# Two halves of one change: a shorter modulation ahead of the scans, and a memory scan whose values carry a column of ones

## The chip, the core and the metric

The kernel runs on one core of a Trainium2 chip, as one program with one launch. The metric is the device time of that core in microseconds, lower is better. Five engines work side by side: TensorE (PE), VectorE (DVE), ScalarE (ACT), GpSimd (POOL) and SyncE (SP), which here issues most transfers. Each has an instruction stream of its own, and semaphores order them.

## What is computed

Two transformer blocks follow each other. Only the first part of the first one is touched: modulation, RMS norm, the input projection, and two bidirectional chunked scans, of which the second (mLSTM, "memory") matters here.

```python
mod_x = (jax.nn.silu(c) @ ada_w + ada_b)[:, None, :]
mod_c = (jax.nn.silu(c_ctx) @ ada_w + ada_b)[None, None, :]
sh1x, sc1x, g1x, sh2x, sc2x, g2x = jnp.split(mod_x, N_MOD, axis=-1)
zx = modulate(rmsnorm(x, norm1_g), sh1x, sc1x) @ w_in
zc = modulate(rmsnorm(ctx, norm1_g), sh1c, sc1c) @ w_in
# memory scan, one chunk, per head
num = qk @ vc + w_inter[..., None] * (qc @ s)
den = jnp.sum(qk, axis=-1) + w_inter * (qc @ n)
h = num / jnp.maximum(jnp.abs(den), jnp.exp(-m_t))[..., None]
s_new = decay[..., None, None] * s + kw.T @ vc
n_new = decay[..., None] * n + jnp.sum(kw, axis=2)
x = x + g1x * mixer_output(gla_hx, ml_hx, ...)
```

Model width 1024, sequence 1024, context 256. `ada_w` is 1024 x 6144, in fp32 24 MB: six vectors of 1024, of which shift and scale of the first norm (`sh1`, `sc1`) are needed first, for x and for the context; the other four (`g1x, sh2x, sc2x, g2x`) only for x, and only behind the scans.

## The kernel before, in words

Everything is fp32; the projections are made of three fp32r products (`product3`, lines 97 to 101) of values split in a rounded high part and a rest. The layout is channels on 128 partitions (`KD = 8` tiles of them) by 1280 tokens (`TOT`, context first), in chunks of 128 (`NCH = 10`, two of context, eight latent).

The order of work is written by hand. The head is a series of stages, each closed by a barrier:

1. `modulation` (line 323). SP loads `ada_w` in 12 slabs of 2 MB (128 partitions x 8 x 512) in a ring of three; TensorE multiplies each with the two columns of `silu(c)` into two rows (8 fp32 matmuls of 512 columns, each two passes); VectorE copies the rows; 48 small transposes turn them into channels.
2. `first_norm` (line 388) loads context, x and gain, and then calls `norm_split` (line 263) once for the context and once for x. There ScalarE squares, TensorE sums the squares over the partitions with a matrix of ones, VectorE makes the reciprocal of the root, multiplies by it (line 315), ScalarE applies gain and shift twice (`y`, and `high` rounded to fp32r, line 291), and VectorE writes the rest `y - high` (line 318).
3. `first_scans` (line 1046) is one stage for the projection and both scans. The projection's weights come in 29 tiles of 512 KB (`Inputs.load`), GpSimd splits each (`Inputs.halve`, lines 446 and 448), TensorE multiplies it by the tokens in pieces of 512, 512 and 256 columns (or 2 x 512 for the gate tiles), 24 passes a piece, and ScalarE takes the bank away (`Inputs.take`). There are 79 pieces. 27 go ahead of the linear scan, 28 in its gaps, 12 between the scans and 12 in gaps of the memory scan, by two tables:

```python
LINEAR_FILLS = [(2, 1)] * 8 + [(1, 1)] * 2
MEMORY_FILLS = [(0, 0, 0)] * 2 + [(1, 0, 0), (1, 1, 0)] * 4
```

The three numbers are pieces in the chunk's three places on TensorE: behind the scores, behind the transposes of k, behind the state's step.

A chunk of the memory scan (`Memory.tensor` from line 881, `Memory.vector` from 952) goes, for both directions d and four heads: TensorE broadcasts rows of gate sums into bank `X[d]` (line 892) and q times k into `Q[d]` (898). VectorE makes the arguments of the exponentials from `X` (971 to 977), ScalarE the exponentials (938 to 940), TensorE transposes k into `X` (904), VectorE weights q, scores and k (982, 985, 988). TensorE makes the output from weighted scores and v and from weighted q and state (914, 915), and the denominator from the same left sides and one column each, `ones1` or `norm` (916, 917), in bank `Dn`. VectorE reads the denominator (991) and scales the output (1000). TensorE makes the state's step (925) and that of `norm` (926); VectorE decays and adds `norm` (1002, 1003) and the state (1005, 1006). The next chunk's rows wait for the state, as they overwrite `X`. Chunks 0 and 1 are of the context and have no output.

Of the kernel before, what the change touches and what calls it, by code (L numbers as in the profile page):

```python
# [8 lines left out]
F32 = mybir.dt.float32  # L9
# [7 lines left out]
P = 128  # L17
# [245 lines left out]
def norm_split(nc, name, src, total, high, rest, gain, shift, ones):  # L263

    cs = chunks_of(total)
    with Stage(nc, name) as s:
        sq = [s.sb(f"sq{j}", [P, BANK]) for j in range(2)]
        rs = s.sb("rs", [P, total])
        t, y = [s.sb(f"t{j}", [P, total]) for j in range(2)], [s.sb(f"y{j}", [P, total]) for j in range(2)]
        ps = [s.ps(f"p{c}") for c in range(len(cs))]  # L270
        squared, used, inverted = s.sem("squared"), s.sem("used"), s.sem("inverted")
        meant, rooted, scaled, gained, left = s.sem("meant"), s.sem("rooted"), s.sem("scaled"), s.sem("gained"), s.sem("left")
        with nc.Block() as block:
            @block.scalar
            def _(act):
                n = 0
                for a, m in cs:
                    for k in range(KD):
                        if n >= 2:
                            act.wait_ge(used, n - 1)  # L280
                        nc.scalar.activation(sq[n % 2][:, 0:m], src[:, k, a:a + m], ACT.Square).then_inc(squared, 1)
                        n += 1
                for c, (a, m) in enumerate(cs):
                    act.wait_ge(meant, c + 1)
                    nc.scalar.activation(rs[:, a:a + m], rs[:, a:a + m], ACT.Sqrt).then_inc(rooted, 1)
                for k in range(KD):
                    act.wait_ge(scaled, k + 1)
                    if k >= 2:
                        act.wait_ge(left, k - 1)
                    for out in (y[k % 2][:], high[:, k, 0:total]):  # L290
                        nc.scalar.activation(out, t[k % 2][:], ACT.Identity, bias=shift(k) if shift else 0.0, scale=gain(k)).then_inc(gained, 1)

            @block.tensor
            def _(pe):
                n = 0
                for c, (a, m) in enumerate(cs):
                    for k in range(KD):
                        pe.wait_ge(squared, n + 1)
                        nc.tensor.matmul(ps[c][:, 0:m], ones[:, 0:P], sq[n % 2][:, 0:m], start=(k == 0), stop=(k == KD - 1)).then_inc(used, 1)
                        n += 1  # L300

            @block.vector
            def _(dve):
                for c, (a, m) in enumerate(cs):
                    dve.wait_ge(used, KD * (c + 1))
                    nc.vector.tensor_scalar(rs[:, a:a + m], ps[c][:, 0:m], 1.0 / D, EPS, ALU.mult, ALU.add).then_inc(meant, 1)
                for c, (a, m) in enumerate(cs):
                    dve.wait_ge(rooted, c + 1)
                    nc.vector.reciprocal(rs[:, a:a + m], rs[:, a:a + m]).then_inc(inverted, 1)
                dve.wait_ge(inverted, len(cs))  # L310
                for k in range(KD + 1):
                    if k < KD:
                        if k >= 2:
                            dve.wait_ge(gained, 2 * (k - 1))
                        nc.vector.tensor_tensor(t[k % 2][:], src[:, k, 0:total], rs[:], ALU.mult).then_inc(scaled, 1)
# [3033 lines left out]
```

## Time and profile before

| | us |
|---|---|
| median of 3 runs (4555.51 to 4556.99) | 4555.62 |
| the profiled execution, its own time | 4557.76 |
| its span | 4556.1 |
| TensorE busy | 3954.2 (87%) |
| VectorE, ScalarE, GpSimd busy | 2163.8, 1493.4, 1078.0 |
| first product of the input projection starts at | 200.92 |
| memory scan, from its first rows to the stage's end | 659.3 to 953.3 |

The profile is of one execution. "Busy" sums the time of instructions on an engine; idle time has a releaser, the instruction or transfer whose semaphore ended it. [...] PE rows count passes: an fp32 matmul shows as two. The numbers behind the name of a line are lines of the kernel before.

### The profile page before, as it was taken

How to read it: one execution, taken by the hardware profiler on the slowest of the kernel's cores; microseconds unless marked ns; L12 is line 12 of the kernel's file. 1: busy time of each engine (PE TensorE's matmuls, PEld its weight loads, DVE VectorE, ACT ScalarE, POOL GpSimd, SP SyncE). 2: the span in 40 equal slices, each digit the busy share in tenths (PEclk: the TensorE clock that was granted, in tenths of full speed). 3: DMA queues.
4: the chain of work that ended last, by engine and by line, in shares of the span. 5: the costliest groups of instructions: out<-in, count | busy, mean ns of one | idle time of the engine just before them, and what ended most of it. 6: DMA issues, size and time to landing. Idle time of an engine off the chain costs nothing. (4 is left out here: it accounts for less than half of the span.)

```text
span 4556.1 us, 45877 instructions
## 1 busy us (share of the span) xinstructions
PE 3954.2 (87%) x17652; PEld 3102.2 (68%) x17652; DVE 2163.8 (47%) x2425; ACT 1493.4 (33%) x1866; POOL 1078.0 (24%) x578
## 2 busy tenths in 40 slices
PE   7499988948549999995788878999979899999998
PEld 1278878836437878775566656777757688888886
DVE  0346734442238888886453422222224564344335
ACT  0332110120227777772422032222222232233233
POOL 0122220013021111103232111222204344444443
PEclk9689987868659999996898789999979999999999
DMA  6131220132249999994232121121115433323323
GB/s 241 67 88 60 76 75 28 38 125 106 84 157 392 395 400 402 400 381 176 94 141 92 37 91 50 66 68 63 62 55 190 142 94 97 97 93 96 98 87 103
DMA packets 152147, 638.80 MB, mean 140 GB/s; under 512 B 18664, under 2 KB 42072, under 8 KB 135344
## 3 DMA queue, kind: packets, MB, share of 16 engines
q1 hardware_dynamic: 121904, 545.89, 33.0%
q10 hardware_dynamic: 20400, 61.35, 3.5%
q0 software_dynamic: 9680, 29.29, 1.7%
q8 instruction: 113, 1.85, 0.2%
q14 instruction: 50, 0.41, 0.0%
HBM read 532.86 MB, written 103.62 MB: 140 GB/s over the span
## 5 line engine op out<-in xcount | busy, mean ns | idle before, releaser
L2990 POOL TENSOR_TENSOR t_wl<-t_raw,t_wh 128x1024 fp32r<-128x1024 f32 (+1 forms) x176 | 397.5, 2262 | 547.1 <-ACT t_wh L3042 547.1
L99 PE MATMUL m_b<-b_high,m_high 128*128 128x512 f32 x960 | 414.6, 432 | 27.0 <-ACT m_ob L1938 19.1
L100 PE MATMUL m_b<-b_rest,m_high 128*128 128x512 f32 x960 | 393.6, 410 | 0.0
L101 PE MATMUL m_b<-b_high,m_low 128*128 128x512 f32 x960 | 384.6, 401 | 0.0
L1909 POOL TENSOR_TENSOR m_high<-m_raw,m_one 128x1024 fp32r<-128x1024 f32 x60 | 115.8, 1931 | 918.1 <-PE m_b L101 864.1
L99 PE MATMUL t_b<-b_high,t_wh 128*128 128x512 f32 x768 | 303.2, 395 | 19.7 <-POOL t_wl L2990 19.5
L100 PE MATMUL t_b<-b_rest,t_wh 128*128 128x512 f32 x768 | 300.7, 392 | 0.0
L101 PE MATMUL t_b<-b_high,t_wl 128*128 128x512 f32 x768 | 300.5, 391 | 0.0
L3042 ACT ACTIVATE t_wh<-t_raw 128x1024 fp32r<-128x1024 f32 (+1 forms) x176 | 175.6, 999 | 343.6 <-PE t_b L101 288.2
L99 PE MATMUL zs_z<-zs_hs,zs_high 128*128 128x512 f32 (+1 forms) x632 | 243.7, 386 | 38.2 <-POOL zs_low L448 38.2
L99 PEld LDWEIGHTS m_b<-b_high,m_high 128*128 128x128 f32 x960 | 187.6, 195 | 89.2 <-ACT m_ob L1938 19.5
L100 PE MATMUL zs_z<-zs_hs,zs_high 128*128 128x512 f32 (+1 forms) x632 | 235.9, 373 | 0.0
L1938 ACT ACTIVATE m_ob<-m_b 128x512 f32<-128x512 f32 x120 | 71.0, 596 | 502.4 <-PE m_b L101 494.9
L101 PE MATMUL zs_z<-zs_hs,zs_low 128*128 128x512 f32 (+1 forms) x632 | 235.1, 372 | 0.0
L100 PEld LDWEIGHTS m_b<-b_rest,m_high 128*128 128x128 f32 x960 | 188.0, 196 | 49.0 <-issue 8.2
L101 PEld LDWEIGHTS m_b<-b_high,m_low 128*128 128x128 f32 x960 | 187.1, 195 | 45.2
L1596 DVE TENSOR_TENSOR ex_wlo<-ex_raw,ex_who 128x2048 fp32r<-128x2048 f32 x78 | 178.7, 2292 | 56.1 <-ACT ex_who L1543 53.9
L99 PE MATMUL t_b<-t_hidh,t_wh 128*128 128x512 f32 x512 | 200.1, 391 | 5.0 <-DVE t_hidl L3139 5.0
L1596 DVE TENSOR_TENSOR ex_wlg<-ex_raw,ex_whg 128x2048 fp32r<-128x2048 f32 x80 | 183.2, 2292 | 43.4 <-ACT ex_whg L1543 43.2
L100 PE MATMUL t_b<-t_hidl,t_wh 128*128 128x512 f32 x512 | 199.9, 390 | 0.0
L101 PE MATMUL t_b<-t_hidh,t_wl 128*128 128x512 f32 x512 | 199.7, 390 | 0.0
L3143 DVE TENSOR_TENSOR t_x<-t_x,t_b 128x512 f32<-128x512 f32 x80 | 54.9, 686 | 290.9 <-PE t_b L101 290.7
(619 smaller groups left out, 9094.5 us busy)
## 6 DMA issues: line engine op xcount, KB each, us to landing
ex_raw<-in_expert_w SPq DMA_DIRECT2D x118, 2048.0 KB, 10.3
t_raw<-in_w_ff SPq DMA_DIRECT2D x128, 512.0 KB, 3.5
m_raw<-in_w_ug SPq DMA_DIRECT2D x60, 512.0 KB, 4.4
ada_w<-in_ada_w SPq DMA_DIRECT2D x12, 2048.0 KB, 7.7
yrows<-ex_y ACTq DMA_DIRECT2D x38, 512.0 KB, 10.9
gates<-m_ob SPq DMA_DIRECT2D x32, 512.0 KB, 2.9
me_g<-gates SPq DMA_DIRECT2D x32, 512.0 KB, 3.7
zs_raw<-in_w_in_s SPq DMA_DIRECT2D x29, 512.0 KB, 3.6
```

Source lines behind the costliest of these rows:

```text
L99: nc.tensor.matmul(out, w[0], x[0], start=first, stop=False)
L100: nc.tensor.matmul(out, w[0], x[1], start=False, stop=False)
L101: return nc.tensor.matmul(out, w[1], x[0], start=False, stop=last)
L1596: V.tensor_tensor(half(wl[u], x_), half(raw[slot], x_), half(wh[u], x_).bitcast(F32), ALU.subtract).then_inc(left, 1)
L1909: g.tensor_tensor(W.high[j][:], W.raw[j][:], W.one[:].broadcast_to([P, D]), ALU.mult).then_inc(W.rounded, 1)
L1938: self.nc.scalar.activation(self.ob[n % 2][:, c * BANK:(c + 1) * BANK], self.banks[m % len(self.banks)][:], ACT.Copy).then_inc(self.taken, 1)
L2990: self.nc.gpsimd.tensor_tensor(self.wl[u % self.NW][:, 0:m], self.raw[u % 2][:, 0:m], self.wh[u % self.NW][:, 0:m].bitcast(F32), ALU.subtr ...
L3042: S.activation(self.wh[u % self.NW][:, 0:m], self.raw[u % 2][:, 0:m], ACT.Copy).then_inc(self.rounded, 1)
L3143: V.tensor_tensor(at, at, b[:], ALU.add).then_inc(self.added, 1)
```

## The change

**The head.** `modulation`, `first_norm` and `norm_split` go. A class `Head` inside the stage of the scans takes their place. It loads context and x (in two halves of 512 tokens) first and then only the first 4 of 12 slabs, as 8 half slabs of 1 MB in a ring of three, with the first two weight tiles of the projection ahead of the last half slab. TensorE multiplies them into four banks; the squares are added by VectorE to one tile `acc`, so TensorE makes one sum of partitions per arrival (256, 512, 512 tokens) in place of eight. x is scaled by the reciprocal root before the modulation is known. Then, piece by piece of the projection (0 to 511, 512 to 1023, 1024 to 1279), VectorE applies gain and shift, ScalarE rounds, and the rest is subtracted by VectorE for even k and GpSimd for odd k. TensorE's first pieces wait for the rest of their own piece alone (`Head.ready`).

**The remaining two thirds** of `ada_w` come through the ring of the weight tiles as 32 quarters of 512 KB (128 partitions x 2 x 512), behind the 29 tiles. VectorE multiplies them by `silu(c)` of x alone (two operations a quarter, four quarters a slab into one of two accumulators), TensorE sums the partitions of each slab with four one-column matmuls, and the bias is added at the end of the scan.

**The memory scan.** v and the state are 129 wide, with a column of ones in v, so the denominator and `norm` are the 129th column of output and state. The fourth head of each direction no longer fits into its bank and goes to `EQ` (outputs, the bank of `Dn`) and `EX` (steps, the third bank of the projection, which has two banks from there on). The state's decay stands ahead of the step's wait, the step counts per direction, and the fills are moved: three pieces in each of chunks 2 to 5, none behind; eight quarters in each of chunks 6 to 9. ScalarE takes its banks behind the exponentials. The diff, cut to its core:

```diff
+class Head:
+    NT, SLABS, RING = 2 * KD, 4, 3
+    PIECES = [(0, BANK), (BANK, BANK), (2 * BANK, CTX)]
+    ARRIVALS = [(0, CTX), (CTX, BANK), (CTX + BANK, BANK)]
...
+    def load(self, sp, between):
...
+        for n in range(2 * self.SLABS):
+            if n >= self.RING:
+                sp.wait_ge(self.used, n - self.RING + 1)
+            if n == 2 * self.SLABS - 1:
+                between()
+            sp.dma_start(self.w[n % self.RING][:], self.A["ada_w"][n // 2][:, n % 2 * 4 * BANK:(n % 2 + 1) * 4 * BANK]).then_inc(self.w_in[n % self.RING], 16)
...
+    def tensor(self, pe):
+        pe.wait_ge(self.silu, 1)
+        mm_ = self.nc.tensor.matmul
+        for n in range(2 * self.SLABS):
+            if n in (1, 2, 3):
+                a, m = self.ARRIVALS[n - 1]
+                pe.wait_ge(self.gathered, (KD - 1) * n)
+                mm_(self.ps[n - 1][:, 0:m], self.C["ones"][:], self.acc[:, a:a + m], start=True, stop=True).then_inc(self.summed, 1)
+            pe.wait_ge(self.w_in[n % self.RING], 16 * (n // self.RING + 1))
+            for x in range(4):
+                k = n % 2 * 4 + x
+                mm = mm_(self.slab[n // 2][0:2, :], self.cs[:, k, :], self.w[n % self.RING][:, x * BANK:(x + 1) * BANK], start=k == 0, stop=k == KD - 1)
+            mm.then_inc(self.used, 1)
...
+    def vector(self, dve):
...
+        for i, (a, m) in enumerate(self.ARRIVALS):
+            dve.wait_ge(self.rooted, i + 1)
+            V.reciprocal(self.rs[:, a:a + m], self.rs[:, a:a + m]).then_inc(self.inverted, 1)
+            dve.wait_ge(self.inverted, i + 1)
+            for k in range(KD):
+                V.tensor_tensor(self.x[:, k, a:a + m], self.x[:, k, a:a + m], self.rs[:, a:a + m], ALU.mult).then_inc(self.scaled, 1)
+        dve.wait_ge(self.c_in, 48)
+        dve.wait_ge(self.turned, 1)
...
     def load(self, sp, n):
-        if n >= 2:
+        if n >= N_Z + 2:
+            sp.wait_ge(self.modulated, 2 * (n - N_Z - 1))
+        elif n >= 2:
             sp.wait_ge(self.split[n % 2], n // 2)
-        sp.dma_start(self.raw[n % 2][:], self.A["w_in_s"][n]).then_inc(self.w_in[n % 2], 16)
+        sp.dma_start(self.raw[n % 2][:], self.A["w_in_s"][n] if n < N_Z else self.rest(n - N_Z)).then_inc(self.w_in[n % 2], 16)
...
+            for x in range(2):
+                k, w, acc = i % 4 * 2 + x, self.raw[n % 2][:, x * BANK:(x + 1) * BANK], self.acc[s % 2][:]
+                dve.wait_ge(self.modulated, 2 * i + x)
+                if k == 0:
+                    self.nc.vector.tensor_scalar(acc, w, self.head.cs[:, k, 0:1], None, ALU.mult).then_inc(self.modulated, 1)
+                else:
+                    self.nc.vector.scalar_tensor_tensor(acc, w, self.head.cs[:, k, 0:1], acc, ALU.mult, ALU.add).then_inc(self.modulated, 1)
...
-MEMORY_FILLS = [(0, 0, 0)] * 2 + [(1, 0, 0), (1, 1, 0)] * 4
+MEMORY_FILLS = [(0, 0, 0)] * 2 + [(1, 1, 1)] * 4 + [(0, 0, 0)] * 4
+MODULATION_FILLS = [(0, 0, 0, 0)] * 6 + [(2, 2, 2, 2)] * 4
```

TensorE, one head's output in the memory scan (`zs_pa` is bank `Q[0]`, `zs_pk` is `Dn`, `ml_v` the values), before:

```order
L914 MATMUL zs_pa<-ml_v,mlb_arg 128x128
L915 MATMUL zs_pa<-mlb_state,mlb_inter 128x128
L916 MATMUL zs_pk<-mlb_ones,mlb_arg 128x1
L917 MATMUL zs_pk<-mlb_norm,mlb_inter 128x1
L914 MATMUL zs_pa<-ml_v,mlb_arg 128x128
```

and now, the same head and the next, and then the step of both directions (`zs_z` is the bank `EX`):

```order
L984 MATMUL zs_pa<-ml_v,mlb_arg 128x129
L985 MATMUL zs_pa<-mlb_state,mlb_inter 128x129
L984 MATMUL zs_pa<-ml_v,mlb_arg 128x129
...
L990 MATMUL zs_pa<-ml_v,mlb_kw 128x129 x3
L990 MATMUL zs_z<-ml_v,mlb_kw 128x129
L990 MATMUL zs_pst<-ml_v,mlb_kw 128x129 x3
L990 MATMUL zs_z<-ml_v,mlb_kw 128x129
```

The one-column matmuls are gone, two a head in the output and one in the step.

VectorE, chunk 6, from the weighted k to the next chunk's first operation (`zs_raw` holds a quarter, `mlb_acc` a slab's accumulator), now:

```order
L1054 SCALAR_TENSOR_TENSOR mlb_kw<-zs_pst,mlb_kd 128x512
L499 SCALAR_TENSOR_TENSOR mlb_acc<-zs_raw,zs_cs,mlb_acc 128x512 x4
L1059 TENSOR_TENSOR mlb_state<-mlb_state,mlb_kd 128x516 x2
...
L1073 TENSOR_TENSOR mlb_o<-zs_pk,mlb_den 128x2x128
L497 TENSOR_SCALAR mlb_acc<-zs_raw,zs_cs 128x512
L499 SCALAR_TENSOR_TENSOR mlb_acc<-zs_raw,zs_cs,mlb_acc 128x512 x3
L1078 TENSOR_TENSOR mlb_state<-mlb_state,zs_pa 128x387
L1078 TENSOR_TENSOR mlb_state<-mlb_state,zs_pst 128x387
L1079 TENSOR_TENSOR mlb_state<-mlb_state,zs_z 128x2x129
L499 SCALAR_TENSOR_TENSOR mlb_acc<-zs_raw,zs_cs,mlb_acc 128x512 x4
```

The decay (L1059) stood behind the step's wait before, and two of the four fills of a chunk show here on both sides of the state's additions.

TensorE, the head now (`hd_w` a half slab, `hd_acc` the added squares):

```order
L344 MATMUL zs_pa<-hd_w,zs_cs 2x512 x4
L340 MATMUL zs_pst<-hd_acc,all_ones 128x256
L344 MATMUL zs_pa<-hd_w,zs_cs 2x512 x4
L340 MATMUL zs_pst<-hd_acc,all_ones 128x512
L344 MATMUL zs_z<-hd_w,zs_cs 2x512 x4
L340 MATMUL zs_pk<-hd_acc,all_ones 128x512
L344 MATMUL zs_z<-hd_w,zs_cs 2x512 x20
L349 MATMUL zs_pa<-all_ident,hd_rows 128x2 x16
```

The third sum stands behind the third half slab, and 32 products of slabs are left of 96.

## Rows read from the trace of the kernel before

**Rows 1.** The page, 40 equal slices of the span, in tenths.
```profile
PE   7499988948549999995788878999979899999998
...
PEclk9689987868659999996898789999979999999999
```
**Rows 2.** Windows by stage: stretch, length, busy PE, PEld, DVE, ACT, POOL, clock, DMA.
```profile
200.90:659.30 458.40, 432.21 (x2236) 355.55 (x2237) 259.05 (x258) 111.50 (x169) 113.53 (x48) 0.95 0.24 81
659.30:953.30 294.00, 263.73 (x1488) 240.66 (x1488) 127.19 (x276) 26.16 (x64) 18.05 (x8) 0.78 0.09 31
```
**Rows 3.** Timeline of the head: start, duration, engine, line, operation, idle before.
```profile
15.12 85.39 PE L358 MATMUL ada_p<-ada_w,ada_cs 128*2 128x512 f32 x192 [15.12 <-DMA ada_w<-in_ada_w]
...
125.93 6.21 PE L299 MATMUL nc_p<-nc_sq,all_ones 128*128 128x256 f32 x16 [20.10 <-ACT nc_sq L281]
...
200.92 0.80 PE L99 MATMUL zs_z<-zs_hs,zs_high 128*128 128x512 f32 x1 [38.18 <-POOL zs_low L448]
...
217.00 0.38 ACT L487 ACTIVATE gla_lr<-zs_z 128x256 f32<-128x256 f32 x1 [2.28 <-PE zs_z L101]
```
**Rows 4.** DMA: GB/s in 40 slices of 105 to 130; issues, median us to landing.
```profile
GB/s 0 0 0 0 0 28 84 293 385 387 378 392 400 419 406 413 413 406 419 406 400 406 400 419 413 413 413 294 7 0 0 0 0 0 0 0 0 0 0 0
...
ada_w<-in_ada_w SPq DMA_DIRECT2D x12, 2048.0 KB, 7.7
zs_raw<-in_w_in_s SPq DMA_DIRECT2D x28, 512.0 KB, 3.6
```
**Rows 5.** Waits in the memory scan: us in total, times, longest.
```profile
PE zs_pa L892 <- DVE mlb_state L1006: 17.1, 9, 1.9
...
DVE mlb_inter L982 <- ACT mlb_inter L938: 54.8, 8, 7.6
DVE mlb_den L991 <- PE zs_pk L917: 54.6, 8, 8.7
```
**Rows 6.** VectorE's timeline, in the norms of the head and in chunk 2.
```profile
133.15 1.75 DVE L309 RECIPROCAL nc_rs<-nc_rs 128x256 f32<-128x256 f32 x1 [0.55 <-ACT nc_rs L285]
134.94 0.76 DVE L315 TENSOR_TENSOR nc_t<-znorm_h,nc_rs 128x256 f32<-128x256 f32 x2
...
163.39 6.55 DVE L309 RECIPROCAL nx_rs<-nx_rs 128x512 f32<-128x512 f32 x2
169.97 2.36 DVE L315 TENSOR_TENSOR nx_t<-znorm_h,nx_rs 128x1024 f32<-128x1024 f32 x2
...
691.04 0.69 DVE L974 TENSOR_TENSOR mlb_inter<-zs_pa,mlb_mbefore 128x512 f32<-128x512 f32 x1
691.76 0.69 DVE L975 TENSOR_TENSOR mlb_arg<-zs_pa,ml_cols 128x512 f32<-128x512 f32 x1
```
**Rows 7.** Two lines, ns min/median/max: VectorE's first tap, GpSimd's subtraction.
```profile
L562 DVE TENSOR_SCALAR glb_out<-glb_pad,zs_cv_w x8: 744/2889/2946, 384.5 to 544.4; 128x1024 f32<-128x1024 f32 x8
...
L448 POOL TENSOR_TENSOR zs_low<-zs_raw,zs_high x29: 2338/2402/4794, 198.5 to 870.5; 128x1024 fp32r<-128x1024 f32 x29
```
**Rows 8.** TensorE in chunk 0: two parts of a step; chunk 1's first rows.
```profile
665.05 0.77 PE L925 MATMUL zs_pa<-ml_v,mlb_kw 128*128 128x128 f32 x2
665.61 0.42 PE L926 MATMUL zs_pk<-mlb_ones,mlb_kw 128*128 128x1 f32 x2
...
673.91 2.07 PE L892 MATMUL zs_pa<-ml_negm,all_ident 64*128 64x128 f32 x8 [1.90 <-DVE mlb_state L1006]
```
**Rows 9.** TensorE in chunk 2: the first and the eighth head's output.
```profile
706.43 0.46 PE L914 MATMUL zs_pa<-ml_v,mlb_arg 128*128 128x128 f32 x2 [1.75 <-DVE mlb_arg L985]
...
706.95 0.28 PE L916 MATMUL zs_pk<-mlb_ones,mlb_arg 128*128 128x1 f32 x2
...
712.67 0.47 PE L914 MATMUL zs_pst<-ml_v,mlb_arg 128*128 128x128 f32 x2
```
**Rows 10.** Windows: chunk 0, and the outputs of chunk 2.
```profile
659.00:672.00 13.00, 12.59 (x56) 11.95 (x56) 2.34 (x8) 0.42 (x2) 0.00 (x0) 0.50 0.00 0
...
708.00:712.00 4.00, 4.00 (x39) 4.00 (x38) 0.68 (x2) 0.00 (x0) 0.00 (x0) 1.00 0.00 0
```

More of the change, by code:

```diff
@@ L260, in _ @@
                     nc.vector.tensor_tensor(dst[:, k, 0:total], src[:, k, 0:total], rs[:], ALU.mult).then_inc(scaled, 1)
[L263 to L278, printed above, removed]
-                        if n >= 2:
[L280 to L315, printed above, removed]
-                    if k:
-                        dve.wait_ge(gained, 2 * k)
-                        nc.vector.tensor_tensor(rest[:, k - 1, 0:total], y[(k - 1) % 2][:], high[:, k - 1, 0:total].bitcast(F32), ALU.subtract).then_inc(left, 1)
-                dve.wait_ge(left, KD)
@@ L423, in __init__ @@
         self.made = self.moved = 0
+        self.first = len(self.pieces) - sum(map(sum, MEMORY_FILLS))
+        self.bank = [i % 3 if i < self.first else i % 2 for i in range(len(self.pieces))]
+        self.modulated, self.reduced, self.biased = s.sem("z_modulated"), s.sem("z_reduced"), s.sem("z_biased")
+        self.quarters = self.sums = 0
         self.rows = [i for i, p in enumerate(self.pieces) if Z_V <= p[0] < Z_MQK or Z_MV <= p[0] < Z_G]
@@ L454, in multiply @@
             pe.wait_ge(self.split[j], n // 2 + 1)
-            if i >= len(self.banks):
-                pe.wait_ge(self.taken, i - len(self.banks) + 1)
-            out = self.banks[i % len(self.banks)][:, 0:m]
+            earlier = [x for x in range(i) if self.bank[x] == self.bank[i]]
+            if earlier:
+                pe.wait_ge(self.taken, earlier[-1] + 1)
+            if n == 0:
+                self.head.ready(pe, i)
+            out = self.banks[self.bank[i]][:, 0:m]
             for k in range(KD):
@@ L879, in late, with four @@
         return slice((ORDER[d][n] - NCC) * CH, (ORDER[d][n] - NCC + 1) * CH)
+    def four(self, bank, four, d):
+        return [bank[:, h * self.W:(h + 1) * self.W] for h in range(3)] + [four[:, d * self.W:(d + 1) * self.W]]
     def tensor(self, pe, fills):
@@ L884, in tensor @@
         pe.wait_ge(self.read, 3)
-        pe.wait_ge(self.start, 5)
+        pe.wait_ge(self.start, 2)
+        pe.wait_ge(self.fourth, 1)
+        pe.wait_ge(Z.taken, Z.first)
         for n in range(NCH):
@@ L933, in scalar @@
             i = n - NCC
-            Z.take(act, fills[n][0])
             for d in range(2):
@@ L1032, in _, with first @@
             def _(sp):
[L1033 to L1034 removed]
+                def first():
+                    Z.load(sp, 0)
+                    Z.load(sp, 1)
+                head.load(sp, first)
                 lin.load(sp)
                 for n in range(N_Z):
[L1037 to L1038 removed]
+                    Z.load(sp, n + 2)
                     if n == 0:
@@ L1048, in _ @@
                         Z.store(sp, n)
+                for n in range(N_Z + 2, N_Z + N_REST):
+                    Z.load(sp, n)
                 for j in range(3):
@@ L1056, in _ @@
                 nc.gpsimd.memset(blank[:], 0.0).then_inc(C["blanked"], 1)
-                Z.halve(pool)
+                Z.fill(pool)
+                Z.halve(pool, range(2))
+                head.gpsimd(pool)
+                Z.halve(pool, range(2, N_Z))
             @block.tensor
             def _(pe):
+                head.tensor(pe)
                 Z.multiply(pe, 4)
```

320 lines of the change are left out of this document (193 added, 127 removed).

## The prediction, made before the changed kernel had run

> **What bounds the kernel now.** I read first the page's slices (114 us each): the second holds 4 tenths of TensorE work at a clock of 0.6, and slices 7 and 8, full of work, run at 0.7 and 0.8 [rows 1]. Then the table by stage [rows 2]: up to 200.9 us the core prepares, from 200.9 to 659.3 it multiplies the input projection (432 of 458 us busy, clock 0.95), and from 659.3 to 953.3 runs the memory scan, 264 of 294 us busy at a mean clock of 0.78. So two places have room: the head, where the first product of the projection starts at 200.92, and the scan, whose slow clock stretches small matmuls.
>
> In the head TensorE's rows [rows 3] tell four steps in series: 192 passes on the modulation's 12 slabs, 15.1 to 100.5 us; their transposes; 20.1 us of waiting for x and context, which are asked for only at 107 us; then sums of squares with waits on ScalarE and, at the end, 38.2 us of waiting for VectorE and ScalarE to scale and split, for a stage change and for the first weights. The transfers are not the limit while TensorE multiplies: 12 slabs of 2.1 MB in 85.4 us are 295 GB/s, and x and context ran at 385 to 419 [rows 4].
>
> In the scan [rows 5] TensorE waits only 1.9 us a chunk for VectorE's state, and VectorE waits for TensorE's outputs (54.6 us over 8 chunks) and for ScalarE's exponentials, 54.8 us, since ScalarE first empties a bank that TensorE fills late. It is a chain that goes to and fro between engines, mostly through TensorE.
>
> **The head, step by step.** The sum runs against the profiled execution (4557.76 us, its span 4556.1; the median of the runs shown, 4555.62, is 2.1 lower).
>
> Transfers: constants, then 5.2 MB of x and context, then 8 half slabs of 1.05 MB, asked for without a gap from 6 to 10 us. By the rate of rows 4 the last x lands at 8 + 2 + 13 = 23 us and the first half slab at 26.
> [...] The first costs 6.8, seven others 3.4 each, the three fp32 sums over `acc` 2.2: 26 + 6.8 + 24 + 2.2 = 59 us. Last move and transposes: turned at 60.4.
> VectorE: the additions to `acc` (21, up to 0.73 each) follow the arrivals and end by 31. The three sums are ready after the third half slab, 42 us; only then come reciprocals (1.75 and 2 x 3.27) and 24 products with `rs` (8 of 256 columns at 0.35, 16 of 512 at 0.60, half of what 1024 take; [rows 6]): 42.8 + 8.3 + 12.7 = 64 us.
> GpSimd splits the first two weight tiles from some 53 us on, 2 x 4.2 us. What VectorE's operations on SBUF do beside it, its convolution's first tap shows: the same 128x1024 tensor_scalar takes 0.74 at least and 2.89 in the median, in chunks where a split of 2.4 starts with it [rows 7]. I charge some 5 us of those 8.4, so VectorE ends at 69, with modulation and gain at 70. VectorE, not the transfers and not TensorE, bounds the new head.
> Piece 0 (256 context and 256 latent columns): 16 tensor_scalar of 0.26 apart, 4 subtractions of 0.60, and 4 of GpSimd at 1.2 (half of its 2.4 for 1024), which I count in series: 11.4. TensorE starts the projection at **82** in place of 200.92. Piece 1 needs 10.3 more, TensorE needs 7.8 for piece 0, so it waits some 2.5 and then some again for piece 2: first tile done at 101 to 104 in place of 217 [rows 3]. That is a gain of 113 to 116; I take **114**. Bounds: without the collision with GpSimd 10 us more (124); with x at half its rate (13 us later, sums later by as much) 101. What goes with it: four stage changes and 8 of 12 slabs, whose work comes back in the scan. From 104 us to the scan nothing else moves: VectorE's mask constants, the four small loads behind the slabs and tile 2's split are all due later than they become ready.
>
> **The scan, step by step.** Per head, the column of ones takes the two one-column matmuls out of the output and one out of the step: a step of 0.85 becomes 0.56 at half clock [rows 8], and an output of 0.89 becomes 0.53 at full clock [rows 9]; twice or half of these stand for the other clock. One column more per matmul I take as nothing (129 for 128). The state's decay moves ahead of the wait, `norm` goes (two operations of 0.16).
> Chunks 0 and 1 now take 14.6 each (from 659.3 to 673.9, [rows 8]). Two row groups 3.9, transposes 1.9, steps 8 x 0.56 = 4.5, and the next chunk may start when VectorE has added d = 0, while TensorE still steps d = 1: 10.5. Gain 8 for both.
> Chunks 2 to 5 carry three pieces each. TensorE's work at full clock: rows and scores 4.2, two transposes 1.1, outputs 8 x 0.53 = 4.2, steps 2.4, three pieces of 24 passes at 0.23 16.5 = 28.4; VectorE's is some 20 and is ready each time before TensorE comes to it (weighed by 12.5 of the chunk, TensorE's outputs begin at 16.3), so there is no gap before which the clock would fall: it stayed 1.00 through outputs that came after a piece [rows 10]. Chunk 2 starts at half clock: 34. Sum 34 + 85 = 119.
> Chunks 6 to 9 have no piece and eight VectorE quarters each. A quarter is two 128x512 operations, 0.73 apart since each waits for the one before (0.69 and the wait, as the last two of rows 6), 64 in all less 8 cheap ones: 46 us. TensorE gets only small fp32 work; such work left the clock at 0.50 in chunk 0, though 12.6 of 13 us were busy [rows 10]. So at half clock a chunk is: state adds 1.0, fill 2.9 and a wait of about 1 for its second transfer (a 512 KB tile lands 3.6 after issue [rows 4], the adds before it cover 1.5), exponents' arguments 5.6, fill 2.9, weighting 3.6, fill 2.9, then a wait of 3.8 until TensorE ends the outputs (8 x 1.1 from the first weighted tile), decay 1.3, denominators and outputs 2.9, fill 2.9, first add 0.6: **31.5**. Chunk 6 still enters warm: 28. Sum 28 + 94.5 = 122.5. Behind the last one its fill is uncovered: 5 + 8 matmuls of 0.28 + the bias = 7.8.
> Scan: 21 + 119 + 122.5 + 7.8 = 270 against 294: **24 less**. Bounds: all transfers of a pair late by 2 us more (16 pairs, 32 us): 8 more than now; half of chunks 2 to 9 faster by the clock (below): 12 less still.
> ScalarE's loads of q and k, which TensorE waits 14.2 us for at 645 to 659, keep their place. The q1 queue gets 30 loads behind `modulated`, and behind them stand only the waits at the stage's end, where nothing else is due. Code after the scan is the same.
> **Sum:** 4557.8 - 114 - 24 = 4419.7, less the 2.1 to the median: **4417.6 us**.
>
> [...] The clock: rows 10 show 0.50 through 13 us in which TensorE was 97% busy with 64- to 128-column fp32 work, so I hold the last chunks at half clock. [...]
>
> **Rivals.**
> *The clock stays high in chunks 6 to 9.* For it: small matmuls after a piece ran at 1.00. Against: chunks 0 and 1. VectorE's 27.7 then bound, 3 x 3.8 less and 1 at the tail: 4405. Chance 0.10.
> *The head gives less.* VectorE's chain starts from the third sum, which waits for TensorE's third half slab; with x slower, TensorE's clock falling in waits for slabs, and GpSimd fully in series in scaling too, the first product starts near 95 and the gain is 100: 4432. For it: the collision rows [rows 7]. Chance 0.15.
> *The quarters stall the scan.* Each buffer is asked for only after its last reader, so a fill can find its second tile absent [rows 4]. At 2 us more a pair, 32 us: 4450. For it: the median of 3.6 holds for a lone load; against: at most two are out and the queue is else empty. Chance 0.08.
> *Slower than before*, by the same mechanism: it decides where every quarter exposes over 138 / 32 = 4.3 us beyond my count. At 7.7 each, as the 2 MB slabs land [rows 4], 32 x 7.7 = 246: 4664. Against it: a quarter is a fourth of such a slab. Chance 0.01.
> *The change doesn't do what it says:* the first product could still wait for all of x to be split, if pieces 1 and 2 were needed at once; they are waited for one by one, so at most 17 us (two pieces of VectorE work less TensorE's 8 and 5.5 under them, some 7 net) are at stake: 4425. In the forecast's range, chance 0.04.
>
> **How the numbers follow.** Forecast 0.62 at 4418. The range holds forecast, warm clock, and late head: down to head 124 and scan 36 less, 4396, and 4 us more for what no row shows: 4392; up to head 100 and scan 12 less (half of the late transfers), 4444, plus 4 for pieces that restart cold: 4448. Outside are the stalled scan and stray, under 0.2. A measurement of this kernel tells 0.2% (9 us) from no change; only stalls of over 130 us reach that: faster 0.97, same 0.01, slower 0.02.
>
> **What would show it.** First L99 product at 76 to 90 us, waiting for VectorE or GpSimd; 32 matmuls (64 passes) of L344 from 26 to 60; GpSimd and VectorE operations stretched around 53 to 100. The scan some 270 long: chunks 0 and 1 near 10.5, 2 to 5 near 28.5 at clock 1.00, 7 to 9 near 31 at 0.50, VectorE's L499 at 0.7 us with waits for zs_raw of under 2 us. I am wrong if the head's end waits on a transfer, if chunks 3 to 5 show a clock of 0.5, if one-column-wider matmuls cost visibly more, or if work behind the scan changes.

## The result and the profile after

| | before | after |
|---|---|---|
| median of 4 runs, us | 4555.57 (4543.32 to 4556.99) | 4388.42 (4385.84 to 4391.55) |
| the profiled execution, its own time | 4557.76 | 4390.69 |
| its span | 4556.1 | 4389.0 |
| first product of the projection starts at | 200.92 | 84.61 |
| first rows of the memory scan at | 659.3 | 549.2 |
| memory scan, to the stage's end | 294.0 | 244.3 |
| from there to the end of the span | 3602.8 | 3595.5 |

The ratio is 0.9639, 95% interval 0.9621 to 0.9658: 167 us faster, where 138 were forecast. The time lies 4 us under the range. The two profiled executions are 167.1 us apart, and the table splits that: **110.1** by the first rows of the scan (forecast 114), **49.7** in the scan (forecast 24), **7.3** behind it (forecast 0).

The page of the changed kernel, to be read against [rows 1], its slices now 110 us each (PEclk, and every clock below, is the one granted to TensorE, 1.00 for full speed):

```profile
PE   4899897285499999967988869999969899999998
DVE  6467457612388888865634332222236473354345
PEclk8899996595599999968997889999979999999999
```

The first slice holds the whole head. The scan lies in slices 6 to 8: its first half now has the clock at 0.9 with TensorE at 9 tenths, and the low digits, 0.6 and 0.5, are its last chunks and the start of the mixer norm, where TensorE has 7 and 2 tenths of work.

Windows by stage, as [rows 2]; the columns are length, then busy time and (count) of PE, PEld, DVE, ACT, POOL, then the granted clock, DMA share and GB/s:

```profile
0.00:84.60 84.60, 33.33 (x86) 7.17 (x87) 56.40 (x77) 24.60 (x42) 15.05 (x14) 0.88 0.53 188
84.60:107.20 22.60, 18.54 (x74) 15.11 (x75) 17.00 (x26) 8.73 (x19) 8.03 (x8) 0.78 0.00 1
107.20:549.20 442.00, 414.38 (x2164) 340.62 (x2162) 258.68 (x256) 110.25 (x167) 110.48 (x46) 0.96 0.25 82
549.20:564.75 15.55, 14.74 (x81) 13.18 (x81) 9.16 (x25) 0.83 (x4) 0.00 (x0) 0.69 0.01 2
564.75:672.74 107.99, 107.99 (x640) 93.67 (x641) 58.28 (x134) 16.58 (x35) 17.34 (x8) 1.00 0.20 66
672.74:696.87 24.13, 13.50 (x90) 12.51 (x89) 20.91 (x44) 3.10 (x7) 0.00 (x0) 0.83 0.43 129
696.87:724.99 28.12, 20.33 (x104) 19.10 (x105) 24.59 (x50) 2.50 (x6) 0.00 (x0) 0.62 0.55 169
724.99:754.32 29.33, 21.62 (x104) 20.38 (x104) 24.60 (x50) 2.50 (x6) 0.00 (x0) 0.62 0.52 161
754.32:793.50 39.18, 24.50 (x120) 22.70 (x120) 28.55 (x56) 2.50 (x6) 0.00 (x0) 0.59 0.49 156
```

From the fourth line on these are chunks 0 and 1; 2 to 5; 6; 7; 8; 9 with the tail. Chunks 2 to 5 take 27.0 each and TensorE is busy for all of 107.99 us at 1.00. In chunks 7 and 8 VectorE is busy for 24.6 of 28 to 29.

The head, in time order. TensorE first, as [rows 3], then VectorE:

```profile
41.60 13.89 PE L344 MATMUL zs_z<-hd_w,zs_cs 128*2 128x512 f32 x32
56.16 3.59 PE L344 MATMUL zs_z<-hd_w,zs_cs 128*2 128x512 f32 x8 [0.67 <-DMA hd_w<-in_ada_w]
59.69 1.17 PE L349 MATMUL zs_pa<-all_ident,hd_rows 2*128 2x2 f32 x16
...
84.61 0.76 PE L99 MATMUL zs_z<-zs_hs,zs_high 128*128 128x512 f32 x1 [23.76 <-POOL zs_hs L404]
...
95.89 0.76 PE L99 MATMUL zs_z<-zs_hs,zs_high 128*128 128x512 f32 x1 [4.05 <-POOL zs_hs L404]
```

```profile
46.78 3.35 DVE L366 RECIPROCAL hd_acc<-hd_acc 128x512 f32<-128x512 f32 x1
50.16 12.60 DVE L369 TENSOR_TENSOR hd_x<-hd_x,hd_acc 128x512 f32<-128x512 f32 x8
62.69 3.34 DVE L366 RECIPROCAL hd_acc<-hd_acc 128x512 f32<-128x512 f32 x1
66.06 4.90 DVE L369 TENSOR_TENSOR hd_x<-hd_x,hd_acc 128x512 f32<-128x512 f32 x8
70.88 0.18 DVE L372 TENSOR_TENSOR all_mod<-zs_pa,zs_bias 128x32 f32<-128x32 f32 x1
```

TensorE has the modulation at 60.9 and waits 23.8 us. The same eight products take 12.60 us once and 4.90 the next time; GpSimd splits its two weight tiles from 52.5 to 62.2 us. So VectorE is done 10 us behind TensorE (70.9), as forecast. The first tile of the projection is done at 107.2; from there to the scan it is 442 us, as before (217.4 to 659.3).

### The profile page after: what moved, and what is told of

It is laid out like the page before. It is cut to its first block and busy times, and to the rows that moved or that the text cites. A ratio compares the mean times of both kernels' runs of the same rounds, so it can differ in the third digit from the quotient of the medians.

```text
span 4389.0 us, 44771 instructions
## 1 busy us (share of the span) xinstructions
PE 3804.7 (87%) x17098; PEld 3014.6 (69%) x17098; DVE 2234.9 (51%) x2546; ACT 1483.1 (34%) x1862; POOL 1092.7 (25%) x590
## 5 line engine op out<-in xcount | busy, mean ns | idle before, releaser
L99 PEld LDWEIGHTS m_b<-b_high,m_high 128*128 128x128 f32 x960 | 187.2, 195 | 89.6 <-ACT m_ob L2029 19.9
## 6 DMA issues: line engine op xcount, KB each, us to landing
ex_raw<-in_expert_w SPq DMA_DIRECT2D x118, 2048.0 KB, 10.2
yrows<-ex_y ACTq DMA_DIRECT2D x38, 512.0 KB, 10.5
```

The source lines that it names most:

```text
L99: nc.tensor.matmul(out, w[0], x[0], start=first, stop=False)
```

## The experiments

Each length of a scan below runs from its first rows to 1.4 us before the first load of the mixer norm is issued, which is the stage's end in the changed kernel too (to VectorE's last operation in the kernel before). All times are single profiled executions unless an interval stands beside them.

**All 12 slabs in the head.** What is the move of 8 slabs worth by itself?

```diff
-    NT, SLABS, RING = 2 * KD, 4, 3
+    NT, SLABS, RING = 6 * KD, 12, 3
-N_REST = 4 * KD
+N_REST = 0
-MODULATION_FILLS = [(0, 0, 0, 0)] * 6 + [(2, 2, 2, 2)] * 4
+MODULATION_FILLS = [(0, 0, 0, 0)] * 10
```

with the rows turned slab by slab, so that they fit in four banks and four slots.

> All 12 slabs in the head (24 half slabs), no quarter in the scan; everything else as changed. Theory (the move of 8 slabs pays because they hide beside the scan's waits): TensorE's slabs go on for 16 x 3.4 = 55 us more, first product near 84.6 + 45 = 130, since VectorE's scaling then hides; chunks 6 to 9 lose most of 8 quarters of 1.5 each and of the tail, 28 -> 18 to 20, so the scan is 244 - 36 to 46 = 198 to 208: the time stays within 10 us of the changed kernel's 4388. Rival (the quarters are nearly free, since the chunk is set by TensorE at half clock and by the way to and fro): chunks 6 to 9 stay at 24 to 28, time 4410 to 4430.

4387.56 us. The first product starts at 134.1, 49.5 later than in the changed kernel, since each slab takes TensorE 7.0 us without a gap:

```profile
60.75 7.03 PE L348 MATMUL zs_pa<-hd_w,zs_cs 128*2 128x512 f32 x16
67.71 0.40 PE L358 MATMUL zs_pa<-all_ident,hd_rows 2*128 2x2 f32 x4
```

Chunks 7 and 8 take 18.3 and 16.1 in place of 28.1 and 29.3, and the scan is 194.9 long, 49.4 shorter. What the head gains by moving the slabs, the scan pays to the microsecond. The theory holds, and it says something on the title: **of the 167 us none comes from the head's loading only a third** (with the quarters where this kernel puts them). They come from the head's new order and from the rewritten memory scan.

**The same, with the 12 pieces at their old places.** The scan then differs from that of the kernel before by the rewritten chunk alone (column of ones, decay ahead of the wait, ScalarE's banks behind the exponentials).

```diff
-MEMORY_FILLS = [(0, 0, 0)] * 2 + [(1, 1, 1)] * 4 + [(0, 0, 0)] * 4
+MEMORY_FILLS = [(0, 0, 0)] * 2 + [(1, 0, 0), (1, 1, 0)] * 4
```

> As the run before, and the 12 pieces back at their old places, one in the even and two in the odd chunks of 2 to 9: so the scan differs from the kernel before by the column of ones alone. Theory (the column and the early decay shorten every chunk by its matmuls): chunks 0 and 1 in 9.5 and 6 as in the changed kernel, chunks 2 to 9 some 4 to 6 us shorter than their 31 to 34 of before, scan about 294 - 13 - 8 x 5 = 240. Rival (the gain in chunks 2 to 5 of the changed kernel comes from three pieces in a row that keep the clock up, not from the column): scan 265 or more.

4405.22 us; scan 211.5, so the chunk's rewriting is worth 82.5 us, far more than the 54 of the theory or the 29 of the rival, and putting the pieces in threes another 16.6 (211.5 to 194.9). Chunk 2 takes 18.8 where it took 31.1.

**The kernel before, kept busy.** How much of the 82.5 is the clock?

```diff
             Z.multiply(pe, fills[n][2])
+            if n < NCH - 1:
+                pe.wait_ge(Z.taken, Z.made - 2)
+                for x in range(8):
+                    self.nc.tensor.matmul(Z.banks[Z.made % 3][:], Z.h[0][:, 0, 0:P], Z.h[0][:, 0, 0:BANK], start=True, stop=True)
```

> The kernel before, with 8 products of 512 columns that nobody reads behind the state's step of chunks 0 to 8, where TensorE waits 1.9 us for the state; nothing else. Question: with the modulation all in the head and the pieces at their old places, the scan with the column of ones is some 214 us long against 294, 80 less, where its matmuls and VectorE's operations left out make some 6 us a chunk. Theory (the rest is the clock: before, every wait of 1.9 us gave back half clock): here the clock is 1.00 through most of the scan and it is 20 to 40 us shorter, without the column. Rival (the column's shorter chain is all of it): chunks keep their 31 to 38 us or grow by the 1.8 us of products: 0 to 16 us longer.

4525.62 us beside 4553.86 for the kernel before on that chip. Its scan is 266.3 in place of 294.0, with 72 products more in it. The same window in a second profile of the kernel before, here, and in the run with the rewritten chunk and the old places:

```profile
656.85:950.80 293.95, 263.67 (x1488) 240.64 (x1488) 127.18 (x276) 26.18 (x64) 18.07 (x8) 0.78 0.09 31
```

```profile
656.39:922.70 266.31, 252.95 (x1560) 228.03 (x1560) 126.08 (x276) 26.17 (x64) 18.07 (x8) 0.89 0.10 34
```

```profile
599.23:811.00 211.77, 186.87 (x1072) 165.83 (x1072) 121.51 (x290) 28.00 (x64) 18.06 (x8) 0.87 0.12 43
```

A wait of 1.9 us at each chunk's end, filled with work nobody needs, gives 28 us. The other 55 come with the shorter chunk, at the same mean clock to within 0.02. TensorE's busy time falls by 66.1 us: the 72 products are 16.6 of them (0.23 each), and the 416 passes left out (1488 to 1072) are 50, or 0.12 us for each one-column pass. Its idle time grows meanwhile, from 13.4 to 24.9. What shares the earlier decay and ScalarE's new order have in keeping it there was not tried apart; VectorE still waits 36.3 us for ScalarE's exponentials in the kept-busy run, and with the new order that wait no longer shows.

**Two pieces in each of six chunks.** Are three pieces a chunk too many?

```diff
-MEMORY_FILLS = [(0, 0, 0)] * 2 + [(1, 1, 1)] * 4 + [(0, 0, 0)] * 4
+MEMORY_FILLS = [(0, 0, 0)] * 2 + [(1, 1, 0)] * 6 + [(0, 0, 0)] * 2
```

> As changed, with two pieces in each of chunks 2 to 7 in place of three in 2 to 5 (stores of the last two gate tiles on ScalarE's queue). Theory (chunks 2 to 5 are TensorE's work, chunks 6 to 9 VectorE's with quarters): 2 to 5 lose a piece of 5.5 each, 27.0 -> 21.5, and 6 and 7 take two pieces in TensorE's waits for 0 to 4 us each more: 14 to 22 us less than the changed kernel. Rival (chunks have a floor from the way to and fro between engines, as the 28 without a piece show): 2 to 5 stay at 25 to 27 and 6, 7 grow to 33: no gain or 5 us more.

4409.49 us, 21 slower than the changed kernel: chunks 2 to 5 take 24.8, 29.6, 28.0 and 29.6 with less work than the 27.0 had. By its length alone the rival has it. The rows at the start of chunk 3 say why:

```profile
587.72 2.05 PE L964 MATMUL zs_pa<-ml_negm,all_ident 64*128 64x128 f32 x8 [3.21 <-DVE mlb_state L1081]
```

**The same pieces, the second behind the step.**

```diff
-MEMORY_FILLS = [(0, 0, 0)] * 2 + [(1, 1, 0)] * 6 + [(0, 0, 0)] * 2
+MEMORY_FILLS = [(0, 0, 0)] * 2 + [(1, 0, 1)] * 6 + [(0, 0, 0)] * 2
```

> As the run with two pieces in each of chunks 2 to 7, the same pieces in the same chunks, but the second behind the state's step in place of behind the transposes. Theory (what made chunks 2 to 5 there 28 in place of 21.5 is the clock: TensorE waits 3.2 us for the state at a chunk's end and is granted half for what follows; a piece behind the step fills that wait): no wait before rows in chunks 3 to 7, clock 1.00 there, 21.5 to 23 each, chunks 6 and 7 set by VectorE at 26 to 28, scan 20 us shorter than the changed kernel's, 42 shorter than that run's. Rival (chunks with two pieces are long for the way to and fro, not for the clock): 27 to 30 again.

4370.77 us, 39 less than that run. Chunks 2 to 5 take 21.7 each. The two stretches, chunks 2 to 5 there and here:

```profile
562.92:674.83 111.91, 99.06 (x545) 87.26 (x545) 57.21 (x133) 14.77 (x32) 16.97 (x8) 0.88 0.17 57
```

```profile
564.48:651.27 86.79, 86.79 (x545) 75.94 (x545) 58.68 (x134) 14.18 (x31) 12.74 (x6) 1.00 0.17 58
```

The same 545 passes in 25 us less. Half of that is clock (99.06 to 86.79 busy), the rest waiting: the piece stands where TensorE would wait for the state. Chunks 6 and 7 take 24.6 and 29.2, VectorE's. The theory holds; what the changed kernel's threes do for chunks 2 to 5, one piece in the third place does.

**Chunks 6 to 8 kept busy.** There TensorE waits 5.3 us each time and starts at half clock, chunk 7 with rows of 2.07 us. Does that cost anything?

```diff
             Z.multiply(pe, fills[n][2])
+            if 6 <= n < 9:
+                pe.wait_ge(Z.taken, len(Z.pieces))
+                for x in range(20):
+                    mm_(Z.banks[0][:], Z.high[0][:, 0:P], Z.h[0][:, 0, 0:BANK], start=True, stop=True)
```

> As changed, with 20 products of 512 columns that nobody reads, into a free bank, behind the state's step in chunks 6 to 8, where TensorE waits 5.3 us for the state. Theory (after that wait the granted clock is half through rows, scores and transposes): chunks 7 to 9 then start at 1.00, rows and scores 4 x 2.07 -> 4 x 1.16, and each is 3 to 6 us shorter: 9 to 18 us less. Rival (VectorE's quarters set the length, whatever TensorE's clock): chunks 7 and 8 stay at 28 to 29, no gain.

4384.88 us. The rows now start warm,

```profile
725.25 1.15 PE L961 MATMUL zs_pa<-ml_negm,all_ident 64*128 64x128 f32 x8 [0.74 <-DVE mlb_state L1082]
```

and chunks 7 and 8 take 28.0 and 27.6 in place of 28.1 and 29.3. The rival holds: with eight quarters in a chunk VectorE's work is the length, and the clock is worth 1.7 us a chunk at most. Probably it is worth nothing: a run below that changes only the head (sums one by one) has no such products, starts the rows of these chunks at 2.07 us, and takes 28.1 and 27.7 for them too. The 3.5 us that this run is faster are no more than such executions differ by.

**Early weight tiles in the head.** Is it GpSimd's split that stretched VectorE's products?

```diff
-            if n == 2 * self.SLABS - 1:
+            if n == 1:
                 between()
```

> As changed, with the projection's first two weight tiles asked for after the first half slab in place of before the last, so that GpSimd splits them beside VectorE's additions and not beside its scaling. Theory (VectorE's scaling of the first latent half took 12.6 in place of 4.9 because GpSimd's split ran beside it): those 8 operations near 5, first product 5 to 8 us earlier less the 2.6 that the slabs come later, time 3 to 7 us less. Rival (the 12.6 has another cause, such as the transfers of slabs into SBUF): they stay over 10, and the time is the same or 3 more.

4381.46 us, first product at 77.8 in place of 84.6. GpSimd now splits from 28.4 to 38.3, and the products of the first latent half are:

```profile
51.18 4.91 DVE L369 TENSOR_TENSOR hd_x<-hd_x,hd_acc 128x512 f32<-128x512 f32 x8
```

The theory holds: 7.7 us of collision. It is not gone but moved: the seven last additions to `acc`, beside the split, take 12.39 in place of 5.47. There it costs 1 us (the third sum ends at 42.7 in place of 41.7), since that sum waits for a half slab anyway.

**Sums one by one, rests on VectorE.** What are VectorE's chain from the third sum and its stretched operations in the pieces worth? The author's estimate was scaling done at 52 to 54, the first product at 72, and 5 us less than the run before.

```diff
             dve.wait_ge(self.summed, i + 1)
             V.tensor_scalar(self.rs[:, a:a + m], self.ps[i][:, 0:m], 1.0 / D, EPS, ALU.mult, ALU.add).then_inc(self.meant, 1)
-        for i, (a, m) in enumerate(self.ARRIVALS):
             dve.wait_ge(self.rooted, i + 1)
...
-                if n % 2:
+                if k:
                     rest(n - 1)
+            rest(i * KD + KD - 1)
...
-                head.gpsimd(pool)
```

> As the run with early weight tiles, and in the head VectorE makes each reciprocal and its 8 products right behind each sum of squares in place of behind the third, and takes over GpSimd's 12 subtractions. [...] Rival (GpSimd did its share for nothing, and VectorE alone is the longer): piece 0 takes 13 or more, pieces 1 and 2 make TensorE wait more than the 4 us it does now, and the time is the same or more.

4370.81 us; first product at 74.4, not 72. The order hardly helped: VectorE's additions, now beside GpSimd's split, last until 38.5,
and the 24.5 us of sums, reciprocals and products behind them end at 63.0, 1.2 earlier than in the run before, not at 53:

```profile
26.15 12.40 DVE L360 TENSOR_TENSOR hd_acc<-hd_acc,hd_sq 128x512 f32<-128x512 f32 x7 [0.70 <-ACT hd_sq L320]
38.47 0.41 DVE L363 TENSOR_SCALAR hd_acc<-zs_pst 128x256 f32<-128x256 f32 x1
```

 Piece 0 is where it gained, 10.5 us in place of 12.8, without GpSimd's subtractions beside it. Not all of this run's gain is its edit's: of the 19.9 us between its profile and the changed kernel's, 10.2 stand at the first product and 3.6 more at the start of the scan, but 3.6 lie in the scan and 2.5 behind it, where no line differs.

**Both together.** Head as above, pieces `(1, 0, 1)` in six chunks.

> The two edits that each gave some 18 us, together: early weight tiles, sums one by one and rests on VectorE in the head; two pieces in each of chunks 2 to 7, one behind the scores and one behind the step. Theory (the head and the scan lie one behind the other): the gains add, 4388 - 18 - 18 = 4351, 4347 to 4355. Rival (they share the cover): 4360 or more.

4365.76 us, so by its number the rival. By its stages the first product stands at 74.7 and the scan is 227.5 long, 3 more than in the run with the pieces alone (chunks 6 and 7: 26.1 and 31.3). Another 7 to 10 are behind the scan, 3602.5 us against 3593 to 3596 in its two parents, and some 6 of the first parent's 18 had been scan and later time that its edit does not touch. That these are an execution's own, the next run makes likely.

**The kernel before, once more.**

> The kernel before, unchanged, for a second profile of it. Question: of the 167 us gained, 7 lie behind the scan's stage, where no line differs (3600.8 us of the span after the stage's end before, 3590.5 to 3593.2 in five kernels with the new head). Theory: it is how one execution differs from another (single runs of before lie between 4543 and 4557), so this profile can show anything from 3588 to 3601. Rival: it belongs to the kernel before (its data or tiles lie elsewhere), and this profile shows 3600 again.

4549.34 us, and from the stage's end on 3596.9 where the first profile had 3602.8; a scan of 293.95 where it had 294.00. So two executions of one kernel differ by 5.9 us behind the scan, where 7.3 are in question, and over the eleven profiles with the new head, whose code there is the same, that stretch lies between 3592.8 and 3602.5. Most of the 7.3 can be chance. That a few belong to the change is not excluded: the three profiles with the old head have 3600 on average, the eleven with the new one 3596. The scan and the head repeat to 0.1 and 2.3 us.

**Buffers of their own for the quarters.** The step from the finding: VectorE bounds chunks 6 to 9 and has room in 2 to 5, but a quarter needs a weight buffer that is free only from chunk 6 on. The fill gets two buffers of 512 columns in the scan's memory, loaded between the last weight tiles, and TensorE sums one slab's accumulator a chunk in place of two (the core of the edit):

```diff
+    def load_rest(self, sp, i):
+        for x in range(2):
+            if 2 * i + x >= 2:
+                sp.wait_ge(self.modulated, 2 * i + x - 1)
+            sp.dma_start(self.slow[x][:], self.rest(i)[:, x * BANK:(x + 1) * BANK]).then_inc(self.slow_in[x], 16)
...
-MODULATION_FILLS = [(0, 0, 0, 0)] * 6 + [(2, 2, 2, 2)] * 4
+MODULATION_FILLS = [(0, 0, 0, 0)] * 2 + [(1, 1, 1, 1)] * 8
```

> As the run with both edits, and the modulation's quarters get two buffers of 512 columns of their own, so that they need not wait for the last weight tile: four quarters in each of chunks 2 to 9 in place of eight in 6 to 9. Theory (in chunks 2 to 7 VectorE has 5 us and more to spare at TensorE's 21.7 a chunk, in 6 to 9 VectorE's 28 bound): chunks 2 to 9 take 22 to 24 each, the scan's last piece of work is no longer than a quarter, and the scan is 15 to 30 us shorter than in that run: near 4330. Rival (quarters lie on the chain to and fro wherever they stand, since TensorE waits for VectorE's weighting and state each time): each costs its 1.5, chunks 2 to 7 grow from 21.7 to 27 and the total does not move; with transfers of 256 KB late, slower.

4339.43 us. Chunks 2 to 8 take 21.7, 23.3, 23.9, 26.5, 23.6, 22.6 and 20.9, the scan 207.3 with all 32 quarters in it:

```profile
532.63:740.20 207.57, 185.84 (x1136) 165.23 (x1136) 171.52 (x355) 28.02 (x64) 19.23 (x8) 0.90 0.39 125
```

That is 12 more than the all-head run's scan without any quarter; but there the pieces stand in threes. Set beside its own pieces, a scan without quarters would be some 183 us, an estimate: 15.4 for chunks 0 and 1, six times the 21.7 of the run with the second piece behind the step, and the 37 of the last two chunks in the all-head run. So the quarters cost some 25 us here. Both engines are over 80% busy. Now the move of 8 slabs out of the head pays, 49 for some 25.

**The last quarter early, timed.** The loads go one quarter ahead as well.

```diff
-MODULATION_FILLS = [(0, 0, 0, 0)] * 2 + [(1, 1, 1, 1)] * 8
+MODULATION_FILLS = [(0, 0, 0, 0)] * 2 + [(1, 2, 1, 1)] + [(1, 1, 1, 1)] * 6 + [(1, 1, 1, 0)]
```

> As the run with own buffers, with five quarters in chunk 2, four in 3 to 8 and three in 9, so that none stands behind the last state: the version that should beat both kernels, timed. Theory: chunk 2 had room (21.7 us, TensorE's), the tail loses the 1.5 of a quarter and part of TensorE's 8 us of waiting for the last sum: 1 to 4 us under the 4339 of that run, 4335 to 4340, 0.952 to 0.953 of the kernel before. Rival (one quarter ahead makes SyncE's queue, which waits for each buffer in turn, late by a transfer in every chunk): DVE waits for mlb_slow grow from 2 us to 8 or more, 4342 to 4350.

4343.3 us median of 5 (4337.59 to 4347.26), ratio 0.9537 to the kernel before, interval 0.9524 to 0.955. The median lies in the rival's range. The run before it, 4339.43, was a single execution, within this one's spread, so between the two it is a draw. The rival's wait is there:

```profile
DVE mlb_acc L504 <- DMA mlb_slow<-in_ada_w: 5.6, 9, 2.0
DVE mlb_kw L1060 <- PE zs_pa L981: 5.5, 3, 2.9
DVE mlb_acc L502 <- DMA mlb_slow<-in_ada_w: 4.8, 6, 1.0
```

10.4 us of waiting for transfers, where the run before had 2.0, go with chunks 2 and 3 of 23.9 and 29.0 us (21.7 and 23.3) and eat the 6 us that the tail gives. The timed version is 45 us under the changed kernel.

## Why the prediction was right, and where it was wrong

The forecast was 29 us too high: the head gave 4 less than forecast, the scan 26 more, and 7 appeared behind it.

**What bounds it, and the head: right.** VectorE, not TensorE and not the transfers, ends the new head. TensorE's modulation was there at 60.9 (forecast 60.4), scaling at 70.9 (69), modulation and gain at 71.7 (70); piece 0 took 12.9 (11.4), the first product came at 84.6 (82), the next piece 4.05 late (2.5), the first tile at 107.2 (101 to 104): 110 of the 114. The term that was short is the collision with GpSimd, charged with 5 of its 8.4 and measured at 7.7. Piece 0 adds 1.5. It is not from the subtractions on GpSimd, which were counted in series at 1.2 each: VectorE's operation of 0.41 took 1.49 to 1.50 each of the three times that one of 1.26 started 0.1 behind it in piece 0. VectorE's own operations stand 0.33 apart, not 0.26. For the 6.8 and 3.4 us of a half slab on TensorE no run shows the value: the changed kernel took 5.03 for the first and 3.47 to 3.60 for the others, and its third sum ended at 41.7 where the forecast had 42.

**"From 104 us to the scan nothing else moves": right**, 442 us both times.

**The scan: mechanism half right, 26 us off.** The chunks' forecast against the trace, in us:

| chunks | forecast | measured |
|---|---|---|
| 0, 1 | 21 | 15.5 |
| 2 | 34 | 27.0 |
| 3 to 5 | 85.2 | 81.0 |
| 6 | 28 | 24.1 |
| 7, 8 | 63 | 57.5 |
| 9 and tail | 39.3 | 39.2 |

The step that failed is the half clock of TensorE's small fp32 work: "10.5" for chunks 0 and 1, "Chunk 2 starts at half clock: 34", and the wait of 3.8 in chunks 7 to 9. Chunks 0 to 2 alone took 42.5 where 55 stood, 12.5 of the 26. The half clock was read from [rows 10], 13 us of chunk 0 at 0.50 with TensorE 97% busy, but it was read for another mixture of work: half of the matmuls in those steps had one column [rows 8], and these are what the change takes out. Without them chunk 0 is at 0.50 for 8.9 us, then at 1.00, and the clock stays there to the end of chunk 5 (1.00 from 558.1 to 672.7):

```profile
549.25:558.10 8.85, 8.76 (x38) 8.16 (x39) 4.10 (x11) 0.42 (x2) 0.00 (x0) 0.50 0.01 2
```

```profile
564.75 1.16 PE L961 MATMUL zs_pa<-ml_negm,all_ident 64*128 64x128 f32 x8 [0.39 <-DVE mlb_state L1078]
```

Eight passes of rows take 1.16 us where the start of chunk 1 took 2.07 [rows 8]. So chunk 0 takes 9.5 and chunk 1 6.1, and chunk 2 too starts warm, not at the 34 of a cold start. Two things set the old chunk apart, the one-column matmuls and the wait of 1.9 at its end. The wait is not all of it: it begins only at 672.0, and the clock of the old chunk was still at 0.50 there, 12.7 us after its first rows, where the new one had risen after 8.9. In all eleven profiles with the new chunk the rows of chunk 1 take 1.15 to 1.35 us, in both of the kernel before 2.07. What it is in the old mixture of work that went with the half clock was not tried apart. The kernel before kept busy, where wide products fill the wait and the one-column ones stay, shows only that both together can be overcome: its rows took 1.50 us in chunk 1 and 1.15 or 1.16 from chunk 2 on. The prediction took one stretch for the behaviour of all small work, though the change altered the very work in it.

Chunks 3 to 5 were TensorE's alone, as forecast, and 1.4 too dear each. For 1.1 of it, a matmul of the output or the step (two passes) starts 0.225 after the one before it, where 0.265 and 0.28 had been taken from rows in which one-column matmuls stood between. Chunk 6 is 3.9 short because, counted from rows to rows, it holds three fills of VectorE and not four. Chunks 7 and 8 fell between forecast and rival. VectorE's chain bounds them (27.7 was the rival's figure, and with the clock kept up they took 28.0 and 27.6). The clock was half through rows and scores, as forecast, but rose within the outputs, and those at half clock took 0.43 a matmul, 0.86 a head, not the 1.1 charged. So VectorE waited 0.2 us for them in chunk 7 and 1.4 in chunk 8, not 3.8. In chunk 7:

```profile
714.71 0.64 PE L985 MATMUL zs_pa<-mlb_state,mlb_inter 128*128 128x129 f32 x2
715.14 0.64 PE L984 MATMUL zs_pk<-ml_v,mlb_arg 128*128 128x129 f32 x2
715.57 0.53 PE L985 MATMUL zs_pk<-mlb_state,mlb_inter 128*128 128x129 f32 x2
715.93 0.39 PE L984 MATMUL zs_pst<-ml_v,mlb_arg 128*128 128x129 f32 x2
716.15 0.39 PE L985 MATMUL zs_pst<-mlb_state,mlb_inter 128*128 128x129 f32 x2
```

Hence 28 to 29, not 31.5. That chunk 9 and the tail came out to 0.1 is partly luck: one transfer came 3.2 us late there, and in two later runs with the same scan, where it was 1.1 to 1.2, this stretch took some 2 us less.

**The quarters.** 46 us and a tail of 7.8 were charged for 32; without them the scan is 49.4 shorter. That is right within 10%, and their waits for transfers stayed at about 1 us each but for that one. What the text never did is to set that price against what leaves the head: it reads "8 of 12 slabs, whose work comes back in the scan" and stops there. The two are equal here.

**Rivals.** None took the forecast's place. The warm clock of the first one came true where it was not asked about, in chunks 0 to 2, and put the time below the range: the scan's bound of 36 less, with "12 less still" for the clock, left the 12.5 us of those three chunks out.

## What to carry to other kernels

Put filler work where an engine waits, not where there is room in the code: the same 12 pieces cost 21 us or gained 18 by their place in the chunk, because the piece behind the step fills a wait and keeps the clock besides (1.00 where it was 0.88 in chunks 2 to 5). Before moving work off the start of a kernel, price it at both ends; it pays only where the receiving engine has slack, and what decides that can be a buffer that comes free late (49 us for 49 here, 49 for some 25 with buffers of its own). A half clock is worth removing where TensorE is the bound (28 us in the kernel before) and little or nothing where another engine is (1.7 us a chunk at most).

## What the runs showed of the hardware

- **Waits and the clock.** In the kernel before, a wait of 1.9 us stood behind every chunk but the last, and half clock behind nearly every wait: the eight passes of rows took 2.07 or 2.08 us behind six of the nine, 1.93 and 1.68 behind two, and 1.20 behind one. With waits of 2.5 the level behind them was mixed: in the run with all slabs in the head and the pieces at their old places, the rows of chunk 4 took 1.15 and those of chunk 5 2.08 behind the same wait. Behind waits of 0.4 to 0.9 it was never half in these runs (rows of 1.15 or 1.16).

```profile
657.69 1.15 PE L970 MATMUL zs_pa<-ml_negm,all_ident 64*128 64x128 f32 x8 [2.49 <-DVE mlb_state L1087]
...
677.25 2.08 PE L970 MATMUL zs_pa<-ml_negm,all_ident 64*128 64x128 f32 x8 [2.49 <-DVE mlb_state L1087]
```

  The wait of 1.9 us is one for VectorE, and filling it gave 28 us.
- **VectorE beside GpSimd.** Eight products of two SBUF tiles took 12.60 in place of 4.90, and seven additions 12.39 in place of 5.47, beside 9.7 and 9.9 us of GpSimd's splits. The prediction charged 5 of 8.4, and the whole of it would have been closer.
- **A column.** At full clock an fp32 matmul of 129 columns, two passes, starts 0.225 us after the one before it, so a pass costs 0.11, and its passes have the 275 ns of those of 128 columns. A one-column pass costs as much, 0.12 us, by the 50 us of busy time that went with 416 of them at a mean clock of 0.9. So here the column that rides along cost nothing that the trace shows (275 ns a pass with it and without), and a matmul of its own for one column cost about as much as one for 129 (at full clock a head's output took 0.89 us with its two one-column matmuls in the kept-busy run and 0.45 without them in the changed kernel): 208 of them were 50 of the 266 us of the kept-busy scan.
